# Output projection of a decoder layer: the 544 token columns cut into 512 and 32 in place of 272 and 272

## The reference

```python
def post_mix(h, o_a, o_b, w_out, g1, b1, g2, b2, wi2, wo2, p, ple_proj, ple_gate):
    o = jnp.concatenate([o_a.reshape(bsz, t, WIDTH_A), o_b.reshape(bsz, t, WIDTH_B)], -1).astype(h.dtype) @ w_out
    h = layer_norm(ALPHA * h + o, g1, b1)
    h = layer_norm(ALPHA * h + 0.5 * swiglu(h, wi2, wo2), g2, b2)
    return h + (p @ ple_proj) * jax.nn.sigmoid(h @ ple_gate)
```

## Time and profile before

| what | value |
|---|---|
| median of 2 runs | 1459.56 us (1458.69 to 1460.43) |
| profiled execution, first to last instruction (span) | 1454.2 us |
| mean granted clock of PE | 0.976 |
| PE busy | 1376.8 us, 95% |
| output projection, chunks 0 to 6 | 902.0 to 947.9 us of the span |

### The profile page before, as it was taken

The page is one execution under the profiler, slowest core; times in us unless marked ns, Lnnn a source line. Parts: engine busy times, 40 slices in busy tenths (PEclk is TensorE's granted clock), DMA queues, the critical chain, the costliest instruction groups (busy, mean ns, idle before and its releaser), DMA issues.

```text
span 1454.2 us, 30740 instructions
## 1 busy us (share of the span) xinstructions
PE 1376.8 (95%) x12059; PEld 1272.3 (87%) x12059; DVE 542.2 (37%) x1340; ACT 455.0 (31%) x841; POOL 615.0 (42%) x423
## 2 busy tenths in 40 slices
PE   7999999999989999999877897989999999999988
PEld 7899999999979879976555666979999999999888
DVE  3222222200243246788899322272222222200444
ACT  4122222211262343257544420162222222211541
POOL 3344444354465645223454004644433334453632
PEclk9999999999999999999989997989999999999989
DMA  7399765766355523332399887444656567665121
GB/s 247 114 259 320 243 211 189 271 229 210 108 181 185 150 83 104 136 113 60 105 284 282 276 298 265 149 135 149 211 189 219 181 220 255 225 218 174 57 71 45
DMA packets 96638, 269.83 MB, mean 186 GB/s; under 512 B 36401, under 2 KB 36786, under 8 KB 96280
## 3 DMA queue, kind: packets, MB, share of 16 engines
q1 hardware_dynamic: 89864, 255.34, 52.4%
q0 software_dynamic: 5632, 10.50, 2.7%
q10 hardware_dynamic: 1040, 2.62, 1.2%
HBM read 259.78 MB, written 109.10 MB: 254 GB/s over the span
## 4 chain that ended last, share of the span: by engine, by line
PE 83%; DVE 8%; POOL 3%; DMA 2%; issue 2%; ACT 2%; SPq 0%; ACTq 0%; DVEq 0%; POOLq 0%
PE bank L1611 22%; PE bank L1615 22%; PE bank L1613 22%; DMA cache_a_ring<-in_cache_a 2%; DVE idx_scores L1453 2%; POOL w_rest L577 2%; PE bank L2154 2%; PE bank L1659 2%; PE bank L1660 1%; PE bank L1661 1%; PE bank L1961 1%; PE bank L1971 1%; PE bank L1983 1%; DVE idx_scores_left L1399 1%; DVE topk_lists L1398 1%
## 5 line engine op out<-in xcount | busy, mean ns | idle before, releaser
L577 POOL TENSOR_TENSOR w_rest<-w_raw,w_high 128x1024 fp32r<-128x1024 f32 (+2 forms) x159 | 410.2, 2580 | 604.4 <-ACT w_high L744 603.4
L744 ACT ACTIVATE w_high<-w_raw 128x1024 fp32r<-128x1024 f32 (+2 forms) x159 | 180.2, 1134 | 766.9 <-PE bank L1615 733.4
L1611 PE MATMUL bank<-x_high,w_high 128*128 128x272 f32 x1808 | 377.5, 290 | 8.7 <-DVE x_rest L1021 8.7
L1615 PE MATMUL bank<-x_high,w_rest 128*128 128x272 f32 x1808 | 374.9, 289 | 0.0
L1613 PE MATMUL bank<-x_rest,w_high 128*128 128x272 f32 x1808 | 373.6, 288 | 0.0
L1611 PEld LDWEIGHTS bank<-x_high,w_high 128*128 128x128 f32 x1808 | 284.7, 189 | 15.5 <-POOL w_rest L577 8.6
L1613 PEld LDWEIGHTS bank<-x_rest,w_high 128*128 128x128 f32 x1808 | 285.0, 189 | 0.0
L1615 PEld LDWEIGHTS bank<-x_high,w_rest 128*128 128x128 f32 x1808 | 283.0, 189 | 0.0
L1053 DVE SCALAR_TENSOR_TENSOR hidden<-silu_gate,bank 128x272 f32<-128x272 f32 x88 | 34.6, 434 | 386.8 <-ACT silu_gate L764 386.8
L1611 PE MATMUL bank<-hidden_high,w_high 128*128 128x272 f32 x616 | 127.7, 288 | 0.0
L1615 PE MATMUL bank<-hidden_high,w_rest 128*128 128x272 f32 x616 | 127.5, 288 | 0.0
(11 more groups left out here) (317 smaller groups left out, 1863.1 us busy)
## 6 DMA issues: line engine op xcount, KB each, us to landing
out_a_sample<-in_cache_a SPq DMA_DIRECT2D x73, 1344.0 KB
w_raw<-in_w_wi SPq DMA_DIRECT2D x88, 512.0 KB, 5.1
cache_a_ring<-in_cache_a SPq DMA_DIRECT2D x112, 384.0 KB, 5.0
w_raw<-in_w_wo SPq DMA_DIRECT2D x32, 704.0 KB, 5.6
w_raw<-in_w_w_in SPq DMA_DIRECT2D x26, 512.0 KB, 3.6
w_raw<-in_w_gate SPq DMA_DIRECT2D x8, 640.0 KB, 3.8
bias_toeplitz<-rev_bias POOLq DMA_DIRECT2D x32, 128.0 KB, 2.7
kv_b_pages<-in_cache_b POOLq DMA_DIRECT2D x64, 64.0 KB, 4.1
```

Of the source, the lines that this page charges most:

```text
L577: nc.gpsimd.tensor_tensor(rest_part(u0, i, j)[:, 0:tiles, :], RAW[:, slot, 0:tiles, :], high_part(u0, i, j)[:, 0:tiles, :].bitcast(F32), A ...
L744: nc.scalar.activation(high_part(u0, i, j)[:, 0:tiles, :], RAW[:, slot, 0:tiles, :], ACT.Copy).then_inc(S["hi_ready"], 1)
L1611: mm(banks[n][:, 0:HALF], wh, xh[n], start=start, stop=False)
L1615: last = mm(banks[n][:, 0:HALF], wl, xh[n], start=False, stop=stop)
```

## The change

Chunks 0 to 6 of the output projection take their columns as 0 to 511 and 512 to 543 in place of 0 to 271 and 272 to 543. `tile` and `unit` get the cut and its widths as arguments, with the old ones for all other callers; `evacuate` uses the new cut for the output projection alone. Chunk 7 (`last_chunk`), the sums and the layer norm stay with halves of 272. The number of matmuls stays 48 for a chunk, and their order over the two column groups too.

```diff
+        def kind(t, k, n):
+            return t[:, k, 0:SEQ] if n == 0 else t[:, k, SEQ:T]
+        KINDS = (SEQ, NDEC)
...
 (evacuate)
+                split, cols = (kind, KINDS) if which == 1 else (half, (HALF, HALF))
                 for n in range(2):
-                    last = v.scalar_tensor_tensor(half(Y, m, n), half(Y, m, n), ALPHA, BANK[2 * (m % 2) + n][:, 0:HALF],
-                                                  ALU.mult, ALU.add)
+                    last = v.scalar_tensor_tensor(split(Y, m, n), split(Y, m, n), ALPHA,
+                                                  BANK[2 * (m % 2) + n][:, 0:cols[n]], ALU.mult, ALU.add)
...
-            def tile(banks, weights, j, xh, xl, start, stop):
+            def tile(banks, weights, j, xh, xl, start, stop, cols=(HALF, HALF)):
                 wh, wl = weights[0][:, j, :], weights[1][:, j, :]
                 for n in range(2):
-                    mm(banks[n][:, 0:HALF], wh, xh[n], start=start, stop=False)
+                    mm(banks[n][:, 0:cols[n]], wh, xh[n], start=start, stop=False)
                 for n in range(2):
-                    mm(banks[n][:, 0:HALF], wh, xl[n], start=False, stop=False)
+                    mm(banks[n][:, 0:cols[n]], wh, xl[n], start=False, stop=False)
                 for n in range(2):
-                    last = mm(banks[n][:, 0:HALF], wl, xh[n], start=False, stop=stop)
+                    last = mm(banks[n][:, 0:cols[n]], wl, xh[n], start=False, stop=stop)
                 return last
...
 (the loop over chunks 0 to 6)
                 unit(u0, m // 4, m % 4, BANK[2 * s:2 * s + 2], OH_, OL_, 0, KD, True, True,
-                     between=mean_between if m == 6 else None).then_inc(S["unit_used"], 1)
+                     between=mean_between if m == 6 else None, split=kind, cols=KINDS).then_inc(S["unit_used"], 1)
```

More of the change, by code:

```diff
@@ L1605, in _, with unit @@
             mm = nc.tensor.matmul
-            def tile(banks, weights, j, xh, xl, start, stop):
+            def tile(banks, weights, j, xh, xl, start, stop, cols=(HALF, HALF)):
                 wh, wl = weights[0][:, j, :], weights[1][:, j, :]
                 for n in range(2):
-                    mm(banks[n][:, 0:HALF], wh, xh[n], start=start, stop=False)
+                    mm(banks[n][:, 0:cols[n]], wh, xh[n], start=start, stop=False)
                 for n in range(2):
-                    mm(banks[n][:, 0:HALF], wh, xl[n], start=False, stop=False)
+                    mm(banks[n][:, 0:cols[n]], wh, xl[n], start=False, stop=False)
                 for n in range(2):
-                    last = mm(banks[n][:, 0:HALF], wl, xh[n], start=False, stop=stop)
+                    last = mm(banks[n][:, 0:cols[n]], wl, xh[n], start=False, stop=stop)
                 return last
-            def unit(u0, i, j, banks, high, low, k0, count, first, last_tile, ready=None, between=None):
+            def unit(u0, i, j, banks, high, low, k0, count, first, last_tile, ready=None, between=None,
+                     split=half, cols=(HALF, HALF)):
                 weights = high_part(u0, i, j), rest_part(u0, i, j)
@@ L1625, in unit @@
                     k = k0 + t
-                    last = tile(banks, weights, t, [half(high, k, n) for n in range(2)], [half(low, k, n) for n in range(2)],
-                                first and t == 0, last_tile and t == count - 1)
+                    last = tile(banks, weights, t, [split(high, k, n) for n in range(2)],
+                                [split(low, k, n) for n in range(2)],
+                                first and t == 0, last_tile and t == count - 1, cols)
                     if between is not None and t < count - 1:
```

## The result

| | before | after |
|---|---|---|
| median | 1459.56 us | 1515.04 us (1514.49 to 1515.59) |
| ratio | | 1.039, 95% interval 1.034 to 1.044 |
| profiled span | 1454.2 us | 1513.9 us |
| first product of the output projection | 902.0 | 904.2 |
| chunk 7 begins | 947.9 | 1010.5 |

The change costs 55.5 us, where 14.5 were forecast and 20.2 was the upper end. The way it went is the rival to which 0.04 was given, the clock. In every execution whose span is known, here and in the experiments, the time lies 1.6 to 1.8 us above the span. So the profiled execution of the kernel before took about 1455.9 us (an estimate) and can't be one of the two behind its median, 1458.69 and 1460.43: of the 5.4 us between 1459.56 and 1454.2 most is the difference between one execution and others.

What follows compares the result with a forecast made beforehand. PE was taken to bound the kernel, busy for 95% of the span. Pair costs and the cold start gave +14.8 us, small waits -0.3, net +14.5 on 1459.6: 1474.1 us, range 1469.6 to 1480.0.

Steps and rivals of the forecast that it cites:

- the clock rival: Output projection: the granted clock falls under the new mix, up to 50 us for the whole stage at half clock; chance 0.04.
- the sum: Output projection: 168 pairs at 0.337 us against 0.250, with a cold start, give +14.8 us; net +14.5.
- the cold stretch: Start of the output projection, 902.0 to about 907.75: 5.8 us at half clock, taken as equally long after the change.
- The cold pair: Output projection at half clock: 0.427 us for 512 columns plus twice 0.112 for the load, 0.651 in all.
- half-cold stage: Output projection with part of the stage at half clock: total time about 1499 us.
- The price of the pair at full clock: Output projection: one 512-column and one 32-column product take 0.225 + 0.112 = 0.337 us, against 0.250 before.
- 512-column product: Output projection at full clock: 0.2136 us for columns plus a fixed 0.0115, so 0.225; bounds 0.214 to 0.235.
- 32-column product: Output projection at full clock: waits for the next weight load, 0.112 us taken; bounds 0.11 and 0.125.
- gap rule: Trainium skill, products at full clock: followed after their columns plus 2.5 ns, never under about 25 ns; change would cost 1.5 us.
- (a), columns only: Output projection: the short product costs its columns only, 0.025 us, so pairs stay at 0.250, time 1459.3 us; chance 0.07.
- (b), two passes: Output projection: short fp32r products run in two passes with two weight loads, +33.4 us, 1492.6 us; chance 0.09.
- The small waits worth 0.3 us: PE's waits at the third chunk and before the last chunk's statistics go, because chunks get longer: together -0.3 us.

Runs made afterwards that it cites:

- experiment 1: The changed kernel with chunk 0 put back to halves of 272, only chunks 1 to 6 with the new cut: 1466.2 us against 1454.4, ratio 1.0076.
- experiment 2: The changed kernel with the short product widened from 32 to 256 columns, the long one unchanged: 1468.3 us, ratio 1.0092 to the kernel before.
- experiment 4: The changed kernel with 24 filler products of 272 columns ahead of its first chunk: 1467.7 us, ratio 1.0102 to the kernel before.
- experiment 5: The changed kernel with 24 filler products of 272 columns ahead of chunk 2: 1487.0 us against 1454.8 for the kernel before, ratio 1.0229.
- experiment 7: The changed kernel with each chunk's 512-column products first and its 32-column ones behind them: 1473.8 us, ratio 1.0140 to the kernel before.
- experiment 9: The kernel before with 12 filler products ahead of the output projection, run twice: 1452.7 us against 1453.6, then 1453.8 against 1454.1.
- experiment 8: The changed kernel unaltered, timed again beside the kernel before on another chip: 1515.1 us, ratio 1.0427.

## Why the prediction was wrong

**The step that failed** is in the sum: "the cold stretch ends at about 907.75, as the average 0.52 over 902 to 908 has it", and then "so 8.9 pairs fit". I took the end of the cold stretch from the kernel before as if it were a time on the clock, and let the new mix run into it. It was a consequence of the products that ran there. With the new mix it did not end for 102.6 us (experiments 1, 2, 4 and 5 show that this is the whole of the surprise). The cold pair itself was priced well, 0.651 forecast and 0.640 measured; only the count was wrong, 8.9 against about 158.

**Why I gave the clock rival 0.04.** The evidence against it was a stretch, 770 to 810, with PE far less busy and the clock at 1.00. That stretch began at full clock. It speaks for "keeps it", which is true, and says nothing on "brings it back", which was the question, as the stage starts cold. The rival was also worded as a fall; what happened is a missing rise. Its price for the whole stage, 159 x 0.314 = 50 us over the warm mix, gives 1524 with the forecast's 14.5, and the measured 1515 is near that. The "half-cold stage" at 1499 was a guess between.

**The price of the pair at full clock** was near: 0.337 forecast, 0.343 measured (1007.03 to 1007.37, and experiment 7). The part that was off is the 512-column product, 0.233 and not 0.225. I read the 0.0115 us beyond the columns as a handover that each product pays once; it grows with the columns (0.125 for 272, 0.233 for 512, 0.46 ns for each column in both). The upper bound 0.235 was the right reading. The 32-column product was right at 0.11, and for the given reason: its rows are as far apart as the weight loads. The Trainium skill (TensorE: Matmul & The Clock Gate, LDWEIGHTS) has a load of 128 columns at 128/1.2 = 107 ns. The trace agrees at full clock, where loads are 0.11 us apart, and not at half clock, where they are 0.21 apart. Its gap rule, cited in the prediction, would have the short product followed after 25 ns and the long after 216; the 0.11 and 0.233 us decide against it for a stream in which every product loads weights. The section from which the prediction took the rule keeps it for single products and gives a stream of loads and products about 131 ns for each product of 512 columns, which the prediction did not say; the 0.233 us disagree with that too.

**With the clock up, the forecast holds, and by half a microsecond only with luck.** The whole change behind fillers costs 14.0 us (experiment 4), where 14.5 were forecast; its interval is 11.6 to 18.2. Experiment 4 has no cold start, which saves the 2.6 us that the kernel before pays for its own, and its pairs are 0.006 us dearer than forecast, 1.0 us in all: two differences that partly cancel. By them the forecast would have been 13.0, inside the interval too.

**The other rivals.** (a), columns only: the 0.11 us rule it out. (b), two passes: the after trace has 56 records for each of the six groups of a line and width, not twice that, so the short fp32r product is one pass.

**The smaller steps.** DVE's evacuation is 0.688 + 0.180 = 0.87 us in place of 0.79, 0.08 more where at most 0.14 was forecast, hidden in full: DVE was idle 86.1 us before the evacuations in these chunks. ACT and POOL wait longer before their splits: 89.6 us before six of ACT's where it was 36.4, and 70.4 before seven of POOL's where it was 17.0. In the up-projection PE is at 1.00 as forecast. The base of the forecast, 1459.6, was the median of two executions and lies about 5 us above the kernel before in the experiments; the sum took the 5.4 us above the span for a part that stays, and what stays is 1.6 to 1.8. The small waits worth 0.3 us can't be told apart in a stage that moved by 60.

## What to carry to other kernels

A clock that comes back by itself in one kernel comes back because of what runs there. When a change puts gaps between matmuls at a place where PE starts at half clock, price the stage at half clock all through beside the other sum, and look for a stretch of the profile that *started* cold with such gaps before setting that aside; a stretch that stayed warm proves nothing. Short products that each load a full weight tile cost the load, 0.11 us at full clock, so cut columns evenly; and if a stage must have such a mix, a few gapless products just ahead of it are cheap: 24 of them, in a wait, were worth 47 us here. They should reach up to the stage: 12 that ended 1.8 us ahead of it (experiment 9) did not keep the clock up.

## What the runs showed of the hardware

- The granted clock has two states that hold themselves under the same load. Pairs of 512 and 32 columns ran for some 100 us at 0.50 without the clock coming back (experiment 8 has it twice), and all 168 of them at 1.00 without it falling, with PE shown as busy for 100% in both.
- At half clock the exposed weight load doubles as the columns do: the pair takes 0.640 us, 512 columns at 1.2 GHz are 0.427 of it, and 0.213 is left. Two loads take 0.54 us there with 0.33 for one, so they are 0.21 apart, against 0.11 at full clock.
- PE's busy time hides this. The granted clock in the table by stretches, and the count of products in a stretch, are what shows it.
- The four passes of the mean sums, 1.6 us of columns without a gap, were followed by the clock's return 1.2 us later; the 24 fillers of 272 columns in experiment 5 had it back at about 935.6, 1.7 us after the first of them.
